# State-space scan passes that give y with features on the partitions, each pair of heads followed by an eighth of the tile's last group

## The reference

```
proj = rms_norm(x) @ W_in                   # q, k, v, u, v_g, z, xBC, dt, gates
A = window attention, B = chunked spatial gating, C = ssd_branch(z, xBC, dt)
h = x + W_out(sig(g_A)*A@P_A + sig(g_B)*B@P_B + sig(g_C)*C@P_C)
out = h + W2 relu(W1 rms_norm(h))^2
```

```
y[l] = sum_{s<=l} (C_l . B_s) exp(acum_l - acum_s) dt_s x_s  +  exp(acum_l) C_l . state
state = state * exp(acum_end) + sum_s exp(acum_end - acum_s) dt_s B_s x_s
y_total = y_forward + y_backward + d_skip * x;   out_C = rms_norm(y_total * silu(z))
```

## Time and profile before

| | |
|---|---|
| median of 3 runs | 2605.32 us (2604.27 to 2605.5) |
| the profiled execution | 2607.9 us, span 2606.1 us |
| PE (TensorE) busy | 2430.2 us, 93% |
| DVE (VectorE) busy | 1204.4 us, 46% |
| ACT (ScalarE) busy | 727.5 us, 28% |
| POOL (GpSimd) busy | 252.7 us, 10% |
| forward pass, first to last TensorE instruction | 809.6 to 1036.8 us |
| backward pass, the same | 1050.4 to 1288.4 us |

### The profile page before, as it was taken

How to read it: one execution, slowest core, us unless ns; L and a number is a source line. 1 busy time by engine, 2 the same in 40 slices (tenths; PEclk the granted TensorE clock), 3 DMA queues, 4 the chain that set the end, 5 groups by cost and what they waited for, 6 DMA issues and landing times. The chain is left out here.

```text
span 2606.1 us, 32797 instructions
## 1 busy us (share of the span) xinstructions
PE 2430.2 (93%) x12924; PEld 2007.2 (77%) x12924; DVE 1204.4 (46%) x1794; ACT 727.5 (28%) x1134; POOL 252.7 (10%) x116
## 2 busy tenths in 40 slices
PE   3999999799997999899749899999999999999999
PEld 1877888576776887788638687878888888888887
DVE  5311264355555776677551386353333333333333
ACT  4421223256652222222160212151212112121120
POOL 3322343000000000000033331000000000000000
PEclk8998999899998999999879999999999999999999
DMA  3122323323234443666424233111111111111112
GB/s 116 37 81 70 120 74 129 105 91 113 89 108 139 157 156 124 196 196 201 152 72 168 99 140 133 41 33 41 35 38 40 40 34 39 40 40 32 40 40 89
DMA packets 142873, 240.39 MB, mean 92 GB/s; under 512 B 9707, under 2 KB 100779, under 8 KB 140108
## 3 DMA queue, kind: packets, MB, share of 16 engines
q1 hardware_dynamic: 142796, 239.34, 27.5%
HBM read 176.99 MB, written 62.32 MB: 92 GB/s over the span
## 5 line engine op out<-in xcount | busy, mean ns | idle before, releaser
L156 PE MATMUL acc<-r_hi,w_hi 128*128 128x512 f32 (+1 forms) x960 | 343.4, 358 | 9.3 <-DVE r_lo L1550 5.8
L157 PE MATMUL acc<-r_hi,w_lo 128*128 128x512 f32 (+1 forms) x960 | 342.2, 356 | 0.0
L158 PE MATMUL acc<-r_lo,w_hi 128*128 128x512 f32 (+1 forms) x960 | 341.5, 356 | 0.0
L157 PE MATMUL acc<-u_hi,w_lo 128*128 128x512 f32 (+1 forms) x768 | 272.4, 355 | 0.0
L156 PE MATMUL acc<-u_hi,w_hi 128*128 128x512 f32 (+1 forms) x768 | 272.1, 354 | 0.0
L158 PE MATMUL acc<-u_lo,w_hi 128*128 128x512 f32 (+1 forms) x768 | 271.6, 354 | 0.0
L1911 DVE TENSOR_TENSOR h_T<-h_T,acc 128x512 f32<-128x512 f32 (+1 forms) x192 | 114.9, 599 | 258.3 <-PE acc L158 258.3
L156 PE MATMUL acc<-xn_hi,w_hi 128*128 128x512 f32 (+1 forms) x624 | 225.1, 361 | 8.5 <-DVE xn_lo L318 8.5
L157 PE MATMUL acc<-xn_hi,w_lo 128*128 128x512 f32 (+1 forms) x624 | 223.3, 358 | 0.0
L158 PE MATMUL acc<-xn_lo,w_hi 128*128 128x512 f32 (+1 forms) x624 | 222.7, 357 | 0.0
L196 ACT ACTIVATE w_hi<-w_raw 128x1024 fp32r<-128x1024 f32 x103 | 108.2, 1050 | 379.3 <-PE acc L158 374.2
(11 more groups left out here) (249 smaller groups left out, 4573.8 us busy)
## 6 DMA issues: line engine op xcount, KB each, us to landing
w_raw<-in_w_tiles SPq DMA_DIRECT2D x146, 512.0 KB, 3.7
h_T<-s_late_T SPq DMA_DIRECT2D x24, 640.0 KB, 5.6
f_w<-s_ac SPq DMA_DIRECT2D x10, 1024.0 KB, 4.9
b_w<-s_ac SPq DMA_DIRECT2D x10, 1024.0 KB, 5.0
s_xbc_T<-x_T_sb SPq DMA_DIRECT2D x12, 640.0 KB, 3.2
s_late_T<-la_result SPq DMA_DIRECT2D x12, 640.0 KB, 3.6
f_xbc<-s_xbc_T SPq DMA_DIRECT2D x10, 768.0 KB, 4.8
b_xbc<-s_xbc_T SPq DMA_DIRECT2D x10, 768.0 KB, 4.9
```

The lines of the kernel that those rows point to most:

```text
L156: pe.matmul(out, w_hi, x_hi, start=first, stop=False)
L157: pe.matmul(out, w_lo, x_hi, start=False, stop=False)
L158: return pe.matmul(out, w_hi, x_lo, start=False, stop=last)
```

## The change

Both passes now give y with features on the partitions: bank_a and bank_b hold, for j = 0 to 7, the 128 features of heads 2j and 2j+1 against the chunk's 128 tokens.

- The product with the state takes the state's 128 columns as weights and C as moving operand: eight matmuls of 128 columns.
- A head's matmul takes the head's 64 columns of `x_dt` as weights and `w` (128 columns) as moving operand. Head 2j writes partitions 0 to 63 of bank_b, head 2j+1 partitions 64 to 127. After each pair comes one eighth of late group 2.
- `turn_y` and `y_turned` are gone; the backward pass gates y in `finish_y`.
- The first half of late group 1 stands ahead of the wait for x_ready.
- exp(acum) has to lie along the tokens now, the same for a head's 64 partitions: `project` computes it for both directions in `copy_rows` (one exp more), sets it to zero in the first chunks (`no_state`), stores it as `grown`, and each pass loads it with two DMAs a chunk, each to 64 partitions.
- The skip term is eight `scalar_tensor_tensor` of 128 columns with d_skip as a factor per partition, in place of two operations over 1024 columns.

```diff
@@ project, SyncE, after the rows' store @@
+                    sp.wait_ge(grown_ok, 2 * d + 2)
+                    sp.dma_start(scratch["grown"][:, d].rearrange("c h t -> h c t"),
+                                 grown[16 * d:16 * d + 16].rearrange("h (c t) -> h c t", c=NT)).then_inc(grown_stored, 16)
@@ project, ScalarE @@
                 def copy_rows(d):
                     act.wait_ge(rows_full, d + 1)
+                    if d:
+                        act.wait_ge(grown_stored, 16 * d)
+                    act.activation(grown, aux[0:32, 0:T], ACT.Exp).then_inc(grown_exp, 1)
                     act.activation(rows[:, d], aux[0:32, 0:T], ACT.Identity).then_inc(rows_read, 1)
@@ project, VectorE, after the first and the second stretch of conv @@
+                def no_state(d):
+                    dve.wait_ge(grown_exp, d + 1)
+                    for c in ((0, SEQ_P // P), (SEQ_P // P - 1, NT - 1))[d]:
+                        dve.memset(grown[:, c * P:(c + 1) * P], 0.0).then_inc(grown_ok, 1)
@@ state_space, load @@
+                    for i in range(2):
+                        sp.dma_start(grown[i * SHD:(i + 1) * SHD, s],
+                                     scratch["grown"][bass.ds(c, 1), int(backward)].rearrange("o (j i) t -> (o i) j t", i=2)[i:i + 1]
+                                     .to_broadcast([SHD, 8, P])).then_inc(loaded[s], 16)
@@ state_space, SyncE's loop @@
-                        sp.wait_ge(y_ready if backward else y_out, n + 1)
+                        sp.wait_ge(y_out, n + 1)
@@ state_space, TensorE @@
                     late.product(pe, s, n, 0)
+                    late.product(pe, s, n, 1, range(KD // 2))
                     pe.wait_ge(x_ready, n + 1)
-                    if backward and not first:
-                        turn_y(1 - s, n - 1)
-                    late.product(pe, s, n, 1, range(KD // 2))
-                    if backward and not first:
-                        pe.wait_ge(turned, n)
                     pe.wait_ge(state_ready, n + 1)
-                    for g in range(SG):
-                        cols = slice(g * 512, (g + 1) * 512)
-                        mm = pe.matmul(bank_a[:, cols], cT[:, g], state[:, cols], start=True, stop=True)
+                    for j in range(8):
+                        cols = slice(j * P, (j + 1) * P)
+                        mm = pe.matmul(bank_a[:, cols], state[:, cols], cT[:, j // 4], start=True, stop=True)
...
-                    for h in range(SH):
-                        cols = slice(h * SHD, (h + 1) * SHD)
-                        mm = pe.matmul(bank_b[:, cols], w[:, s, h], x_dt[:, cols], start=True, stop=True)
-                        if h == SH - 1:
-                            mm.then_inc(y_full, 1)
-                        if h % 2 == 0:
-                            late.product(pe, s, n, 2, [h // 2])
+                    for j in range(8):
+                        for i in range(2):
+                            h = 2 * j + i
+                            mm = pe.matmul(bank_b[i * SHD:(i + 1) * SHD, j * P:(j + 1) * P], x_dt[:, h * SHD:(h + 1) * SHD],
+                                           w[:, s, h], start=True, stop=True)
+                        if j == 7:
+                            mm.then_inc(y_full, 1)
+                        late.product(pe, s, n, 2, [j])
@@ state_space, VectorE @@
                     if backward:
                         dve.tensor_tensor(y[:, s], y[:, s], other[:, s], ALU.add).then_inc(y_ready, 1)
+                        gate(s, n)
                     else:
-                        dve.wait_ge(skip_ready, n + 1)
-                        dve.tensor_tensor(y[:, s], y[:, s], skip[:], ALU.add).then_inc(y_out, 1)
+                        for j in range(8):
+                            cols = slice(j * P, (j + 1) * P)
+                            step_of = dve.scalar_tensor_tensor(y[:, s, cols], xbc[:, s, j], d_col[:, j:j + 1], y[:, s, cols],
+                                                               ALU.mult, ALU.add)
+                        step_of.then_inc(y_out, 1)
...
-                    dve.tensor_tensor(heads(y[:, s]), heads(bank_a[:]), over_dims(factor(s, S_UPTO)), ALU.mult).then_inc(y_scaled, 1)
+                    dve.tensor_tensor(y[:, s], bank_a[:], grown[:, s].rearrange("p j t -> p (j t)"), ALU.mult).then_inc(y_scaled, 1)
...
-                    if backward and not is_first(n):
-                        gate(1 - s, n - 1)
-                    if not backward:
-                        dve.wait_ge(row_in, 16)
-                        dve.tensor_tensor(heads(skip[:]), heads(x_tok[:, s]), over_dims(d_row[:]), ALU.mult).then_inc(skip_ready, 1)
```

More of the change, by code:

```diff
@@ L346, in project @@
         scan = sb("scan", [P, NT, N_SCAN, 32])
-        rows = squares[0:32]
+        rows, grown = squares[0:32], x_T[0:32, 7]
         dt_ln = sb("dt_ln", [P, NT, 32])
@@ L383, in project @@
         sums_full, sums_read, sums_exp, scan_ok = (sem(n) for n in ("sums_full", "sums_read", "sums_exp", "scan_ok"))
-        rows_full, rows_read, rows_stored = (sem("ac_" + n) for n in ("rows_full", "rows_read", "rows_stored"))
+        rows_full, rows_read, rows_stored, grown_exp, grown_ok, grown_stored = (sem("ac_" + n) for n in (
+            "rows_full", "rows_read", "rows_stored", "grown_exp", "grown_ok", "grown_stored"))
         XBC_CUTS = (0, 3, 5, 6)
@@ L698, in _ @@
                         scan_factors()
+                    if at < 2:
+                        no_state(at)
 class LateTiles:
@@ L1211, in state_space @@
         factors = sb("factors", [P, 2, N_SCAN, 32])
+        grown = sb("grown", [P, 2, 8, P])
         if backward:
             other = sb("other", [P, 2, HW])
-            y_fm = sb("y_fm", [P, 2, HW])
             z = sb("z", [P, HW])
         else:
-            skip = sb("skip", [P, HW])
-            d_row = sb("d_row", [P, SH])
+            d_col = sb("d_col", [P, 8])
         x_tok = sb("x_tok", [P, 2, HW])
@@ L1245, in state_space @@
         passed = sem(tag + "passed")
[L1246 to L1251, removed]
+        (col_in, z_in, x_full, bc_full, x_ready, c_read, seg_ready, exp_done, x_end_ready, x_dt_ready, w_ready,
+         kept_ready, start_full, state_full, state_ready, y_scaled, y_full, y_added, y_ready, y_out) = (
+             sem(tag + n) for n in (
+                 "col_in", "z_in", "x_full", "bc_full", "x_ready", "c_read", "seg_ready", "exp_done", "x_end_ready",
+                 "x_dt_ready", "w_ready", "kept_ready", "start_full", "state_full", "state_ready", "y_scaled", "y_full",
+                 "y_added", "y_ready", "y_out"))
         def chunk_of(n):
@@ L1257, in is_first @@
             return isinstance(n, int) and n == 0
-        loads = 16 * (3 if backward else 2)
+        loads = 16 * (5 if backward else 4)
         with nc.Block() as block:
@@ L1323, in _ @@
                 if not backward:
-                    sp.wait_ge(row_in, 16)
+                    sp.wait_ge(col_in, 16)
             @block.tensor
             def _(pe):
[L1328 to L1333, removed]
                 def step(s, n, came):
@@ L1396, in decays_of_pairs, with step @@
                     act.activation(w[:, s], w[:, s], ACT.Exp).then_inc(exp_done, 1)
[L1398 to L1404, removed]
+                def step(s, n, more=True):
                     act.wait_ge(x_full, n + 1)
@@ L1419, in _ @@
                 decays_of_pairs(0, 0)
[L1420 to L1430, removed]
+                step(0, 0)
+                step(1, 1)
+                with act.Fori(1, NT // 2 - 1) as pair:
+                    for s in range(2):
+                        step(s, pair * 2 + s)
+                step(0, NT - 2)
+                step(1, NT - 1, False)
             @block.vector
@@ L1438, in gate @@
                     dve.wait_ge(z_in, n * 16 + 16)
-                    dve.wait_ge(turned, n + 1)
-                    dve.tensor_tensor(y_fm[:, s], y_fm[:, s], z[:], ALU.mult).then_inc(y_out, 1)
+                    dve.wait_ge(y_ready, n + 1)
+                    dve.tensor_tensor(y[:, s], y[:, s], z[:], ALU.mult).then_inc(y_out, 1)
                 def segments(s, n, came, sums):
@@ L1481, in step @@
                     dve.wait_ge(start_full, n + 1)
-                    if stores is not None and not backward:
+                    if stores is not None:
                         dve.wait_ge(y_stored[s], stores)
-                    dve.tensor_tensor(heads(y[:, s]), heads(bank_a[:]), over_dims(factor(s, S_UPTO)), ALU.mult).then_inc(y_scaled, 1)
+                    dve.tensor_tensor(y[:, s], bank_a[:], grown[:, s].rearrange("p j t -> p (j t)"), ALU.mult).then_inc(y_scaled, 1)
                     dve.wait_ge(state_full, n + 1)
@@ L1487, in step @@
                     dve.tensor_tensor(state[:], kept[:], bank_b[:], ALU.add).then_inc(state_ready, 1)
-                    if backward and not is_first(n):
-                        gate(1 - s, n - 1)
-                    if not backward:
```

(8 more changed lines are left out.)

11 lines of the change are left out of this document (5 added, 6 removed).

## The result

The changed kernel takes **2628.64 us** (median of four runs, 2627.99 to 2629.58), the kernel before on the same chip 2605.41 (2604.27 to 2607.43): a ratio of 1.0089 with a 95% interval of 1.0071 to 1.0106, 23.2 us slower. The forecast was 2623 us. The profiled execution takes 2627.99 us (span 2626.2), 20.1 us more than that of before; the sum had said 18.0.

What follows compares the result with a forecast made beforehand. Both passes were taken as bound by TensorE's start-to-start distances, with waits at the stage edges. The terms 19.0 + 1.0 - 7.9 + 3.8 - 2.6 + 4.7 = +18.0 us gave 2623 us from the median, own range 2613 to 2633.

Steps and rivals of the forecast that it cites:

- Heads: Both passes: a group of two heads and a late eighth takes 0.91 us instead of 0.80; +19.0 us over twenty steps.
- Rival 1: Heads: packing pays, way into and out of the halves hidden behind late matmuls; 160 groups save 22 us, 2582 us; 7%.
- Product with the state: Both passes: sixteen instructions of 128 columns take 1.77 us instead of four of 512 in 1.72; +1.0 us.
- Transposes of y: Backward pass: dropping them saves 0.88 us in each of nine steps; -7.9 us.
- Pass starts: Start of each pass: `grown` loads queue ahead of the running sums, 1.9 us each; +3.8 us for two passes.
- Pass ends: Ends of passes: forward +0.3 us from the skip term, backward -2.9 us from a shorter chain; together -2.6 us.
- Projection: Projection stage: second row copy waits for the `grown` store, TensorE idles 2.8 us, clock drops, one more store; +4.7 us.
- Covered work: Inside the steps: moved gate, eight skip operations and added DMAs stay covered by TensorE; uncovered, up to 1.2 us a step.

Runs made afterwards that it cites:

- the own row: Changed kernel with the second direction's exp(acum) in a tile of its own, so its copy of rows waits for no store: 2621.42 us.
- the kernel with all edits: Changed kernel with all pairs of heads in a row, the second exp in its own tile and the `grown` loads behind the running sums: 2567.15 us.
- the late loads: Changed kernel with the loads of `grown` queued behind the running sums, with a semaphore only the start of y waits for: 2632.98 us.

## Why the prediction was right, and where it was off

The mechanism was right, and the sum, 18.0 us, was 2.1 us short of the 20.1 by which the profiled executions differ. That it came so close is in part luck: the projection was 3.6 us dearer than forecast, the two passes together 1.6 us (14.9 for 13.3), and attention and all that follows the passes, for which the sum had no term, were 3.1 us shorter. The medians differ by 3.1 us more than the profiled executions, since the one of before lay 2.5 us above its median and the one of after 0.7 below.

- **Heads** (+19.0 forecast): right, by the row it was taken from. The attention stage's group gave 0.91 us, the trace of after 0.93, so eight groups are 1.0 us a step instead of 0.95. The experiments add what no row of before could: the price is 0.35 us a passage there and back. Of these, 0.10 us are the way in and 0.25 the way out. The rule cited from the Trainium skill, "TensorEngine Tiling (Array Packing)", Key Properties, that changing the mode drains the engine, agrees in that each passage costs time. That a drain is what takes it, no run shows by itself. Rival 1, packing pays, was wrong for groups of four but right for the idea: with 32 in a row it is what makes the kernel 2576 us.
- **Product with the state** (+1.0): sixteen instructions of 128 columns take 1.79 us from L1370 at 1018.53 to L1378 at 1020.32, as against 1.77 forecast and 1.72 before.
- **Transposes of y** (-7.9): right. A backward step had 0.89 us more than a forward one; now the two are equal.
- **Pass starts** (+3.8): right in sum. From the first load of x to the first segments it is 10.87 and 12.30 us, 1.8 later each than the earlier trace rows, 1.9 forecast. The price of the loads alone is another: 2.3 and 3.1 us by the run without them. Something that no term had makes up for 0.6 and 1.3 us of it, so the agreement is in part luck. On the forward VectorE timeline and SyncE's:

```profile
821.25 4.19 DVE L1443 TENSOR_SCALAR f_w<-f_w,f_factors 128x128 f32<-128x128 f32 x16 [10.08 <-DMA f_w<-s_ac]
```

```profile
810.38 0.43 SPq L1289 DMA_DIRECT2D f_xbc<-s_xbc_T  x1
...
811.64 1.38 SPq L1293 DMA_DIRECT2D f_grown<-s_grown  x2
813.06 0.77 SPq L1284 DMA_DIRECT2D f_w<-s_ac  x1
```

- **Pass ends** (-2.6): the chain through TensorE and ScalarE is three operations of VectorE now, 3.8 us as forecast, the gate directly behind the sum of both y:

```profile
1308.33 1.22 DVE L1448 TENSOR_TENSOR b_y<-b_y,b_bank_b 128x1024 f32<-128x1024 f32 x1 [8.41 <-PE b_bank_b L1387]
1309.59 1.22 DVE L1451 TENSOR_TENSOR b_y<-b_y,b_other 128x1024 f32<-128x1024 f32 x1
1310.92 1.23 DVE L1435 TENSOR_TENSOR b_y<-b_y,b_z 128x1024 f32<-128x1024 f32 x1
```

- **Projection** (+4.7): the mis-sized term; it measured +8.3. The wait itself ended where it was forecast, at 454.41 (454.3). But one table load only was counted, on the way back; the other, ahead of exp, is missing from the sum. The trace has it behind the wait (454.41, 1.28 us), so the first evacuation is at 459.36 and not at 457.8. The last tile's first matmul on TensorE's timeline, and its last:

```profile
460.10 0.76 PE L156 MATMUL acc<-xn_hi,w_hi 128*128 128x512 f32 x1 [4.75 <-ACT x_T_sb L556]
...
476.68 0.28 PE L158 MATMUL acc<-xn_lo,w_hi 128*128 128x256 f32 x1
```

The last matmul of the same tile before the change, whose first is in the earlier trace rows:

```profile
469.28 0.28 PE L158 MATMUL acc<-xn_lo,w_hi 128*128 128x256 f32 x1
```

The window behind the wait of 4.75 us (columns as in the earlier trace rows):

```profile
459.00:466.00 7.00, 5.90 (x14) 4.68 (x15) 4.38 (x6) 3.77 (x6) 2.03 (x1) 0.52 0.00 0
```

TensorE waited 4.75 us, not 2.8, and the tile began 4.5 us later than before (460.10 and 455.62). At the lower clock its first 6 us were slow, so from its first matmul to its last it took 16.6 us instead of 13.7: 2.9 us lost, where 3 us at the lower clock and a loss of 1.5 were forecast. The second store of `grown` at the stage's end cost 0.9 us, 0.4 forecast. That makes 4.5 + 2.9 + 0.9 = 8.3 us. Attention, whose code is unchanged, was 1.9 us shorter in that profile. Its length goes with the stretches at the lower clock in its first 40 us (leaving out one that reaches over from the projection): 6.8 us of them and 321.2 us in the changed kernel, 10.2 and 323.1 before, 13.6 and 324.2 with the own row. Whether the stall in the projection shortens attention is not shown: four of the seven traces with that stall have 10.2 us and 322.6 to 323.2, about as before, and the kernel with all edits, which lacks the stall, has 6.8 and 321.3.

- **Covered work**: no wait of TensorE inside the steady steps of either pass, as forecast.

## What to carry to other kernels

Putting two products side by side in the halves of the array pays only over a run of them: here 0.11 us a pair of instructions is won against 0.35 us for each way there and back, so group all half-width work of a step and let whole-width work follow in one piece. Look for the price of a switch in a row that holds a whole group with its neighbours, not in the spacing inside it. When a wait is put ahead of an instruction that needs a table load, count the load behind the wait.

## What the runs showed of the hardware

A table load stood behind the wait of the activation that needs it, although ScalarE had been idle for 4.95 us (454.41); in the seven traces with that wait the idle time is 4.93 to 4.98 us and the load behind it 1.28. And an earlier start of TensorE can be lost again, or more: with the late loads it began the first step of the backward pass 2.7 us earlier, 2.3 us of waiting in that step were followed by 14 us at a granted clock of 0.52, and the pass was 4.1 us longer than in the changed kernel, which waited 0.2 us at the same place and kept 1.00. A wait of that length did not always do it: 2.75 us in the forward pass of the same run left the clock at 1.00, and 2.55 us in the run with all edits were followed by 3.4 us at 0.50.
